# A mixture-of-experts backbone: down weights in 8 KB runs of two rows a partition, and a product of silu and up with a column step of two

## What is computed

```
hid = silu(x @ w_gate[e]) * (x @ w_up[e])     # 1024 -> 512 hidden columns
y   = hid @ w_down[e]                         # 512 -> 1024
```

## Time and profile before

| | |
|---|---|
| three executions, median | 1229.22 us |
| the profiled execution | 1220.43 us |
| its span, first to last instruction | 1218.7 us |
| granted TensorE clock, mean | 0.963 |
| TensorE matmul busy | 1073.9 us (88%) |
| VectorE busy | 534.0 us (44%) |
| ScalarE, GpSimd busy | 207.8 us (17%), 179.0 us (15%) |
| weights' queue q1 | 288.98 MB |
| down loads | 32 of 2 MB, 16 a layer |

### The profile page before, as it was taken

How to read it: one execution, slowest core, us unless ns; L and a number is a source line. 1 busy time by engine, 2 the same in 40 slices (tenths; PEclk the granted TensorE clock), 3 DMA queues, 4 the chain that set the end, 5 groups by cost and what they waited for, 6 DMA issues and landing times.

```text
span 1218.7 us, 36590 instructions
## 1 busy us (share of the span) xinstructions
PE 1073.9 (88%) x15056; PEld 664.2 (54%) x15057; DVE 534.0 (44%) x1510; ACT 207.8 (17%) x555; POOL 179.0 (15%) x229
## 2 busy tenths in 40 slices
PE   3899989999799889999877489999998899998876
PEld 0444444445444477877666344444445787776652
DVE  0236653446316754444333371304467444444327
ACT  1222243334212100000000151101220000000010
POOL 0001200000000021222111250410002222222121
PEclk9899999999899899999998799999989999999888
DMA  8932289998142469599999776116063969999964
GB/s 316 383 124 88 84 291 349 325 377 345 59 116 109 173 265 417 223 420 417 421 420 418 254 251 236 69 69 241 35 240 129 419 236 418 415 422 420 420 233 172
DMA packets 97183, 329.72 MB, mean 271 GB/s; under 512 B 15561, under 2 KB 28273, under 8 KB 88817
## 3 DMA queue, kind: packets, MB, share of 16 engines
q1 hardware_dynamic: 65632, 288.98, 60.6%
q10 hardware_dynamic: 25168, 20.71, 5.5%
q0 software_dynamic: 6336, 19.41, 4.4%
HBM read 312.27 MB, written 25.18 MB: 277 GB/s over the span
## 4 chain that ended last, share of the span: by engine, by line
PE 61%; DMA 19%; DVE 9%; issue 3%; SPq 3%; ACT 2%; ACTq 1%; POOL 0%; POOLq 0%; DVEq 0%
PE PS L1460 15%; PE PS L1470 9%; DMA ring<-in_e_down_dram 9%; PE PS L1286 8%; PE PS L1535 8%; PE PS L1387 7%; PE PS L1307 4%; PE PS L1216 3%; DMA RFW<-in_e_down_dram 3%; DMA expert_rows<-RE 3%; PE PS L1318 2%; DVE mx L870 2%; DMA ring<-in_w_ada_dram 2%; DMA fold_rows<-fsh 1%; SPq L337 1%
## 5 line engine op out<-in xcount | busy, mean ns | idle before, releaser
L1460 PE MATMUL PS<-ring,RE 128*32 128x128 f32 x7040 | 210.4, 279 | 32.0 <-DMA ring<-in_e_up_dram 18.2
L1460 PEld LDWEIGHTS PS<-ring,RE 128*32 128x32 f32 x7040 | 201.9, 113 | 45.3 <-issue 40.4
L1470 PE MATMUL PS<-ring,RE 128*32 128x256 f32 x1760 | 115.9, 382 | 6.1 <-DMA ring<-in_e_down_dram 3.0
L682 ACT ACTIVATE RE<-PS 128x64 f32<-128x64 f32 x160 | 35.7, 223 | 472.8 <-PE PS L1460 435.3
L1387 PE MATMUL PS<-ring,UR 128*128 128x512 f32 x256 | 112.9, 595 | 1.9 <-ACT G L643 1.1
L1127 DVE TENSOR_TENSOR RE<-RE,PS 128x64 f32<-128x64 f32 x160 | 35.4, 221 | 177.6 <-ACT RE L682 177.6
L1535 PE MATMUL PS<-ring,UR 128*128 128x512 f32 x256 | 110.8, 593 | 2.6 <-ACT UR L724 2.6
L1460 PE MATMUL PS<-UR,RE 128*32 128x128 f32 x3072 | 95.2, 283 | 10.8 <-DMA UR<-in_e_up_dram 8.5
L1460 PEld LDWEIGHTS PS<-UR,RE 128*32 128x32 f32 x3072 | 91.1, 114 | 15.8 <-issue 12.8
L1286 PE MATMUL PS<-ring,UR 128*128 128x512 f32 x224 | 98.4, 593 | 0.7 <-ACT UR L571 0.7
L482 POOL DMA_INDIRECT RE<-tokens,gcol x80 | 79.6, 996 | 60.3 <-POOL gcol L496 60.3
(11 more groups left out here) (257 smaller groups left out, 1105.6 us busy)
## 6 DMA issues: line engine op xcount, KB each, us to landing
ring<-in_w_ada_dram SPq DMA_DIRECT2D x24, 2048.0 KB, 11.5
ring<-in_e_down_dram SPq DMA_DIRECT2D x22, 2048.0 KB, 28.4
ring<-in_e_gate_dram SPq DMA_DIRECT2D x22, 2048.0 KB, 19.2
ring<-in_e_up_dram SPq DMA_DIRECT2D x22, 2048.0 KB, 23.4
UR<-in_e_up_dram SPq DMA_DIRECT2D x10, 2048.0 KB
RFW<-in_e_down_dram SPq DMA_DIRECT2D x10, 2048.0 KB
UR<-in_e_gate_dram SPq DMA_DIRECT2D x10, 2048.0 KB
expert_rows<-RE ACTq DMA_DIRECT2D x320, 32.0 KB
```

What stands on the lines that cost most here:

```text
L682: A(gs[:, 64 * h:64 * h + 64], PS[:, h, 0:64], ACT.Silu).then_inc(silu_rd[l], 1)
L1460: ins = mm(PS[BLK * q:BLK * q + BLK, h, 0:P].rearrange("p (g b i) -> p g b i", g=2, b=2), xT[:, k, :], wgu[:, :, k, 2 * h:2 * h + 2, q, :] ...
L1470: ins = mm(PS[BLK * q:BLK * q + BLK, 5, 0:256], hidT[:, BLK * k:BLK * k + BLK], wd[:, k, 256 * q:256 * q + 256], start=(k == 0), stop=(k = ...
```

## The change

The down weights of an expert are loaded with rows 2p and 2p+1 of each half of 256 on partition p: runs of 8 KB instead of 4 KB, 256 of them instead of 512. Partition p of the down operand then holds hidden columns 256h + 2p + r. To match, the gate and up product takes 64 consecutive weight columns per column group instead of two pieces of 32, and the product of silu and up writes its output in the order (r, i) while it reads both inputs with a step of two columns. The numbers of instructions, their sizes, waits and order stay as they are.

```diff
@@ load_expert (SyncE)
-                    src = e_down[l, e].rearrange("(k p) n -> p k n", p=P)
-                    dst = dst.rearrange("p (k n) -> p k n", k=FC)
+                    src = e_down[l, e].rearrange("(h p r) n -> p h (r n)", h=2, r=2)
+                    dst = dst.rearrange("p (h n) -> p h n", h=2)
                 sp.dma_start(dst, src).then_inc(w_in[b], 16)
@@ the loop over blocks (VectorE)
-                            V_.tensor_tensor(hid[:, cut], gs[:, cut], PS[:, h, 64:128], ALU.mult).then_inc(loop, 1)
+                            V_.tensor_tensor(hid[:, cut].rearrange("p (r i) -> p r i", r=2),
+                                             gs[:, cut].rearrange("p (i r) -> p r i", r=2),
+                                             PS[:, h, 64:128].rearrange("p (i r) -> p r i", r=2), ALU.mult).then_inc(loop, 1)
@@ expert (TensorE)
-                    wgu = pair.rearrange("p g (k b q i) -> p g k b q i", k=DC, b=FC, q=CG)
+                    wgu = pair.rearrange("p g (k h q c) -> p g k h q c", k=DC, h=2, q=CG)
...
-                                    ins = mm(PS[BLK * q:BLK * q + BLK, h, 0:P].rearrange("p (g b i) -> p g b i", g=2, b=2),
-                                             xT[:, k, :], wgu[:, :, k, 2 * h:2 * h + 2, q, :], start=(k == 0), stop=(k == DC - 1))
+                                    ins = mm(PS[BLK * q:BLK * q + BLK, h, 0:P].rearrange("p (g c) -> p g c", g=2),
+                                             xT[:, k, :], wgu[:, :, k, h, q, :], start=(k == 0), stop=(k == DC - 1))
```

## The result

The changed kernel takes 1232.45 us (median of 7 runs, 1232.03 to 1234.75) against 1229.22 us (7 runs, 1226.45 to 1231.42) of the kernel before: ratio 1.0032, 95% interval 1.0017 to 1.0046. It is slower by about 3.2 us.

A forecast was written before the change was run, and what follows sets the result against it. TensorE's pace was taken to bound each layer until its unbroken weight stream begins, then the stream's bytes. Late stores of 5.1 us less 1.9 of shorter loads gave +3.2 us on 1229.22: 1232.4 us, range 1226.5 to 1235.5.

The forecast's parts named there:

- late stores: Block stores delayed by larger weight packets, ahead of and inside the weight stream of both layers: 5.1 us slower in all.
- Shorter down loads: Down loads in each layer's weight stream: 8 KB packets save 0.12 us a load, eight loads a layer, 1.9 us in all.
- rival 4: Down loads: the 8 KB runs are moved as 4 KB packets, no change at all, 1229.2 us; chance 0.05.
- Late stores ahead of the stream: Before each layer's weight stream: stores get fewer turns, TensorE waits, and the stream starts 1.9 us later in either layer.
- Stores inside the stream: Early in each layer's stream: late stores delay a weight issue, leaving the engines idle 0.9 us in layer 0, 0.4 in layer 1.
- The product: Product of silu and up on VectorE: reading with a step of two costs 0, at most 42 ns a product.
- the rival built on it: Product of silu and up: its PSUM step costs 1.3 us on top, 1233.7 us; chance 0.05.
- Gate and up matmuls: Gate and up matmuls on TensorE: 128 columns in two runs of 64 instead of four of 32 cost 0.
- rival 2: Expert stages: stores catch up in pauses, all 20 down loads gain, -2.4 to -3.0 us, about 1226.5; chance 0.18.
- Rival 1: Expert stages: each stall relieves the next, half of the 5.1 us remains, +0.6 us, 1229.8, no change; chance 0.30.

The follow-up runs named there:

- e8: The whole change against the kernel before, on a chip with 6.0 us blocks: 1231.82 us against 1227.58, ratio 1.0035.
- e7: The kernel before, unchanged, on a chip with 6.0 us blocks: 1228.2 us against 1227.58, ratio 1.0009.
- e2: Only the down load changed to 8 KB runs, against the kernel before, on a chip with 5.44 us blocks: 1221.31 us, ratio 1.0014.
- e4: Only the product of silu and up changed to the step of two, against the kernel before: 1218.26 us, ratio 0.9992.
- e1: The kernel before, unchanged, on a chip with 5.44 us blocks: 1219.14 us against 1219.7, ratio 0.9996.

## Why the prediction was right, and where it was not

**The number** (1232.4 us, measured 1232.45; slower) is right. Its working is right only in part, and that the sum met the median within 0.1 us is luck: 5.1 us of late stores, of which at most 0.9 are seen, stood where 4.8 us of a late start belonged, a term that the prediction does not have; and 1.9 us of gain stood for about 0.9.

**Shorter down loads, -1.9 us: right in kind, about half in size.** From the opening of the stream to its last landing e8 needs 1.30 us less than e7 in layer 0 and 0.55 in layer 1, 1.85 in all; I had 0.96 in each. But this is the pair with the largest gain. Over all profiles with 6.0 us blocks the six with 8 KB packets take 169.8 us on average in layer 0 and 170.4 in layer 1, the three with 4 KB 170.4 and 170.8: 0.9 us in all. Where blocks take 5.44 us, e2 gains nothing in layer 0 (169.5 us, against 168.7 to 169.3 in the 4 KB profiles) and 1 us or more in layer 1 (169.4 against 170.4 and 170.9). The packet itself was sized well: 307 ns, I had 315 from a line between 4 and 16 KB. Queue q1 has 57440 packets in e8 and 65632 in e7, the 8192 fewer that were foretold: rival 4, 8 KB runs moved as 4 KB packets, is out.

**Late stores ahead of the stream, +1.9 us in each layer: nothing of it is clear of the scatter.** The opening issue came 0.85 and 0.05 us later (e8 against e7, from the first block and from that of layer 1). With the blocks of 5.44 us that the prediction was made for, it came 66.3 us behind the first reload in layer 0 of e2 and 65.1 in layer 1, and the four 4 KB profiles have 64.9 to 67.6 and 65.2 to 65.8. The rule behind the term holds, one packet for one packet, and on the first chip the waits for stores grew by half, from 36.4 to 54.0 us over both layers. What failed is the step from the earlier trace rows to TensorE: I took 1.0 us of hidden lateness against waits that were 0.9 us late already, and added backlog over three experts; the longer waits of e2 stayed hidden. On the timed chips the premise was gone as well, since a block takes 6.0 us there, the stores come further apart and L1133 waits for them for 10.7 us in all in e7.

**Stores inside the stream, +0.9 and +0.4 us:** nothing of it shows. The first issue of gate weights to UR behind the opening came 35.71 us after it in e7 and 35.79 in e8, and 34.09 in e2 against 33.15 to 34.06 in the four 4 KB profiles with the same block.

**The product, 0: right,** in e4 and in every profile (221 or 222 ns), and the rival built on it is out. The row I took it from for SBUF does not bear it, though. The L855 of 426 ns is the first of a pair; the second of each pair takes 1.49 us, with GpSimd's L472 running beside it, and all 16 of that size have a mean of 958 ns. It is e4 that shows the step to be free, for the SBUF input as for PSUM. The Trainium skill (Advanced Engine Details and Errata, Memory Cachelines) wants pairs of PSUM elements side by side; here a step of two over PSUM had no price on VectorE that 1 ns would show.

**Gate and up matmuls, 0:** their mean is 277 ns (from the ring) and 273 ns (from UR) in e8 against 274 and 276 in e7, no difference by the trace. The kernels with the matmuls alone leave the question open in the way told above.

**The missing term, +4.8 us.** I read the load at L337 as one that runs in the stream. "No step is moved past another queue" was true and beside the point: the same edit also changes the static loads ahead of layer 0, and one of them has a critical load on the other queue for company. The chain of waits of before has both pieces:

```profile
332.64 10.71 DMA LB<-in_ln_b_dram
...
345.66 18.04 DMA fold_rows<-fsh
```

I had read the end of that chain only. With the rule I already had, one packet for one, 16 turns longer by 315 - 162 = 153 ns would have given 2.4 us there, against 2.2 measured. TensorE's clock, 1.7 us, has no term in the prediction at all.

**The rivals.** For the expert stage rival 2 (the later landing stays hidden, the loads gain) comes closest: no cost of the stores is clear, and the gain is 0.9 us where it had 2.4 or more. By itself that would have made the kernel faster. The rule cited for it, turns of many descriptors, is refuted by the counts 142 to 146 and 242 to 242. Rival 1 (each stall relieves the next) leaves half of the 5.1 us, 2.5; e8 shows 0.9 in its two layers and e2 nothing clear.

**Profile and median.** I carried over the 8.8 us between the profiled execution and the median as a constant. By the times and the blocks they were a difference of chips: of the 10.0 us between the spans of e1 and e7, 9.0 lie in the two expert stages.

## What to carry to other kernels

When a DMA engine shares itself packet for packet, the size of a packet is a price set on everybody else. Larger packets make their own transfer quicker and every transfer beside them slower, most of all one of small packets. So list every place where the edited load is issued, the few static ones too, and ask at each of them what else is in flight and who waits for it. Where a wait grows ahead of dense matmuls, count the clock's fall behind it as well; and where a transfer is moved out of one collision, look at what it meets next.

## What the runs showed that I had not expected

- The same kernel has 5.44 us blocks on one chip and 6.0 us blocks on another (e1 and e7); in total it takes 1219.7 us on the first and 1227.6 to 1229.6 us on three others. The 0.56 us are a stop of TensorE near the end of a gate and up group, or at the start of the down group behind it, whose releaser the trace doesn't show. Stretches of 128x512 matmuls have no such stop (in 728 to 822 us of e7 all its gaps of over 0.1 us come to 0.11 us).
- A store packet of 4 bytes takes a turn as one of 4 KB does (242 against 242). The four vectors of `fold_rows` need 17.7 to 20.4 us even with few weights beside them, and 27.2 and 28.6 us with them.
- TensorE's clock stayed up behind waits of 0.6 to 2.4 us before L1368 and fell for 3.4 us behind those of 3.2 to 4.6 us.
